# RWKV-7 in a two-block kernel: dense 64x64 products on all four quarters of the array, and the next quarter's k and r projections moved between them

## What is computed

```python
def wkv7_scan(r, w, k, v, a, b):
    def step(state, inp):
        r_t, w_t, k_t, v_t, a_t, b_t = inp
        sa = jnp.einsum('bhvk,bhk->bhv', state, a_t)
        state = (state * w_t[:, :, None, :] + sa[..., None] * b_t[:, :, None, :]
                 + v_t[..., None] * k_t[:, :, None, :])
        return state, jnp.einsum('bhvk,bhk->bhv', state, r_t)

def rwkv7_time_mix(z, mu, w0, w2, a0, a2, g2, k_k, k_a, r_k, ln_w, ln_b):
    z = z + (prev - z) * mu                      # prev: z one token earlier
    r, k, v, wd, ad, gd = split_cols(z, RWKV_SPLIT)
    decay = jnp.exp(-jnp.exp(-jax.nn.softplus(-(w0 + jnp.tanh(wd) @ w2)) - 0.5))
    a, g = jax.nn.sigmoid(a0 + ad @ a2), jax.nn.sigmoid(gd) @ g2
    kk = heads(k * k_k); kk = kk / jnp.maximum(jnp.sqrt(jnp.sum(kk * kk, axis=-1, keepdims=True)), 1e-12)
    k = k * (1.0 + (a - 1.0) * k_a)
    y = wkv7_scan(r_h, heads(decay), k_h, v_h, -kk, kk * a_h)
    # group norm of y by head, plus bonus = sum(r * k * r_k) * v, times g
```

## Time and profile before

| | us |
|---|---|
| timed runs, median of 3 | 1599.73 (1595.28 to 1599.88) |
| profiled execution | 1595.0 |
| its span | 1593.2 |
| TensorE busy in the span | 1540.0 |
| VectorE, ScalarE, GpSimd busy | 893.0, 695.6, 120.5 |

### The profile page before, as it was taken

The page is one execution under the profiler, slowest core; times in us unless marked ns, Lnnn a source line. Parts: engine busy times, 40 slices in busy tenths (PEclk is TensorE's granted clock), DMA queues, the critical chain, the costliest instruction groups (busy, mean ns, idle before and its releaser), DMA issues.

```text
span 1593.2 us, 33669 instructions
## 1 busy us (share of the span) xinstructions
PE 1540.0 (97%) x14522; PEld 1272.5 (80%) x14522; DVE 893.0 (56%) x1645; ACT 695.6 (44%) x1268; POOL 120.5 (8%) x86
## 2 busy tenths in 40 slices
PE   7999989899999999999998999999999999999998
PEld 5787757779789797887887777888887888888887
DVE  3658364656374574842245998433346677777323
ACT  5543265563352633523234998422235433333222
POOL 0004000002230322402000000000000000000000
PEclk9999989999999999999999999999999999999999
DMA  6322303431020110206312000223342323323231
GB/s 220 107 80 80 107 26 104 152 106 37 9 75 11 54 36 24 60 11 148 80 53 80 2 2 2 93 88 98 106 141 84 106 85 100 105 81 106 68 124 74
DMA packets 110947, 124.41 MB, mean 78 GB/s; under 512 B 21288, under 2 KB 94632, under 8 KB 110416
## 3 DMA queue, kind: packets, MB, share of 16 engines
q1 hardware_dynamic: 107872, 114.85, 23.3%
q10 hardware_dynamic: 2928, 7.41, 1.4%
HBM read 118.04 MB, written 4.21 MB: 77 GB/s over the span
## 4 chain that ended last, share of the span: by engine, by line
PE 76%; DVE 13%; ACT 5%; issue 3%; SPq 1%; DMA 1%; POOL 0%; DVEq 0%; ACTq 0%; POOLq 0%
PE bank L801 72%; PE bank L811 3%; ACT arena L1481 3%; DVE arena L2079 2%; DVE weights_lo L2076 2%; DVE arena L2076 2%; DVE ff_c L2079 1%; ACT L1481 1%; DVE ff_c L2076 1%; DVE act_lo L2076 1%; DVE arena L2083 1%; ACT weights_hi L1481 1%; DVE ff_c L2084 1%; DVE arena L2247 1%; DMA arena<-in_c_rwkv 1%
## 5 line engine op out<-in xcount | busy, mean ns | idle before, releaser
L1481 ACT ACTIVATE arena<-bank 128x512 f32<-128x512 f32 (+4 forms) x419 | 225.9, 566 | 564.7 <-PE bank L801 542.9
L801 PE MATMUL bank<-h_hi,weights_hi 128*128 128x512 f32 (+1 forms) x1008 | 402.4, 399 | 9.4 <-DVE weights_lo L2076 6.8
L2076 DVE TENSOR_TENSOR weights_lo<-weights,weights_hi 128x1024 fp32r<-128x1024 f32 (+1 forms) x190 | 239.6, 1261 | 305.2 <-ACT weights_hi L1481 298.2
L801 PE MATMUL bank<-h_lo,weights_hi 128*128 128x512 f32 (+1 forms) x1008 | 394.5, 391 | 0.0
L801 PE MATMUL bank<-h_hi,weights_lo 128*128 128x512 f32 (+1 forms) x1008 | 394.2, 391 | 0.0
L801 PE MATMUL bank<-arena 64*64 64x64 f32 (+7 forms) x7746 | 345.7, 247 | 16.3 <-ACT arena L1481 6.8
L801 PEld LDWEIGHTS bank<-arena 64*64 64x64 f32 (+3 forms) x7746 | 281.8, 140 | 71.2 <-issue 57.1
L1481 ACT ACTIVATE weights_hi<-weights 128x1024 fp32r<-128x1024 f32 (+1 forms) x190 | 200.2, 1054 | 167.1 <-PE bank L801 164.3
L801 PEld LDWEIGHTS bank<-h_hi,weights_hi 128*128 128x128 f32 (+1 forms) x1008 | 190.1, 189 | 60.2 <-DVE weights_lo L2076 14.2
L801 PEld LDWEIGHTS bank<-h_hi,weights_lo 128*128 128x128 f32 (+1 forms) x1008 | 190.2, 189 | 40.7
L801 PEld LDWEIGHTS bank<-h_lo,weights_hi 128*128 128x128 f32 (+1 forms) x1008 | 190.4, 189 | 37.3
(11 more groups left out here) (172 smaller groups left out, 1662.9 us busy)
## 6 DMA issues: line engine op xcount, KB each, us to landing
weights<-in_w_in SPq DMA_DIRECT2D x41, 1024.0 KB, 5.4
weights<-in_ffn_up SPq DMA_DIRECT2D x22, 1024.0 KB, 5.1
weights<-in_ffn_down SPq DMA_DIRECT2D x10, 1024.0 KB, 5.0
weights<-in_w_out SPq DMA_DIRECT2D x8, 1024.0 KB, 5.2
weights<-in_w_in SPq DMA_DIRECT2D x16, 256.0 KB, 4.6
weights<-in_w_branch_rwkv SPq DMA_DIRECT2D x4, 1024.0 KB, 5.2
weights<-in_w_branch_nsa SPq DMA_DIRECT2D x4, 1024.0 KB, 5.1
arena<-in_x SPq DMA_DIRECT2D x4, 512.0 KB, 6.3
```

Of the source, the lines that this page charges most:

```text
L801: return pe.matmul(o, w, x, start=first, stop=last)
L1481: return act.activation(o, i, f, **kw)
L2076: return dve.tensor_tensor(o, a, b, op)
```

## The change

The two head parities x (even and odd heads) become the two halves of each dense product, in place of the two halves g of the tiles. `product` takes even heads on quarters (0,0) and (1,1) and, where `cross` is set, odd heads from one half to the other, (0,1) and (1,0); the odd heads' matrices then lie in turned halves after one product and back after the next. For the parity that ScalarE reads, the old value is added on TensorE with one more product, by ident, behind each (`plus`). `ta` becomes 32 products by ident instead of 8 transposes and goes ahead of pa; `w` goes by parity too; the odd heads' first gram block is written as two products of 64 columns. ScalarE and VectorE read one parity each. GpSimd's operations are whole instead of halved, and its start of the inverse turns the odd heads.

k0, k1 and r0 of the next quarter are made in steps (`more`) at 15 places between gram and gates, r1 beside the states where k0 was. These four jobs use the last bank alone; the others go round the other seven within RWKV. The head of quarters 1 to 3 keeps v0, ss, out, v1 and kk, in this order; in it the `kk` products now stand in v1, behind the output transposes. Quarter 0's head stays, and quarter 3 has no steps.

```diff
+        beside = set()
+        first_of_rwkv = total[0]
         for q in range(4):
             if q == 0:
                 job(q, "k", 0)
             twice(q, "decay", "a")
-            job(q, "k", 1)
-            job(q, "r", 0)
-            job(q, "ss")
-            job(q, "r", 1)
-            twice(q, "kk")
-            job(q, "v", 0)
-            if q:
+            if q == 0:
+                job(q, "k", 1)
+                job(q, "r", 0)
+                job(q, "ss")
+                job(q, "r", 1)
+                twice(q, "kk")
+                job(q, "v", 0)
+                job(q, "v", 1)
+            else:
+                job(q, "v", 0)
+                job(q, "ss")
                 twice(q - 1, "out")
-            job(q, "v", 1)
+                job(q, "v", 1)
+                twice(q, "kk")
+            if q < 3:
+                for kind, n in (("k", 0), ("k", 1), ("r", 0), ("r", 1)):
+                    job(q + 1, kind, n)
+                    beside.add(J[q + 1, kind, n])
             twice(q, "tb", "tk", "low")
             for c in range(TT):
                 for x in range(2):
                     job(q, "gram", c, x)
             twice(q, "tv")
             job(q, "bonus")
...
+            for kind, lev in (("ta", None), ("pa", 0), ("pb", 0), ("pa", 1), ("pb", 1), ("pd", 1), ("pa", 2), ("pd", 2),
+                              ("pd", 3), ("mu", 0), ("mx", None), ("my", 0), ("mz", None), ("mu", 1),
+                              ("x0", None), ("my", 1)):
+                for x in range(2):
+                    job(q, kind, x, *(() if lev is None else (lev,)))
             for g in range(2):
...
+                for x in range(2):
+                    job(q, "w", x, g)
             for g in range(2):
                 for z in range(2):
                     job(q, "e", g, z)
             job(q, "g", 0)
             twice(q, "s")
             job(q, "g", 1)
...
             twice(q, "y")
             job(q, "st")
+        last_of_rwkv = total[0]
...
+        places, times, turn_of = [], [0] * BANKS, 0
+        for j in range(total[0]):
+            if j < first_of_all_banks:
+                b = j % FEW_BANKS
+            elif j in beside:
+                b = BANKS - 1
+            else:
+                if turn_of % BANKS == BANKS - 1 and first_of_rwkv <= j < last_of_rwkv:
+                    turn_of += 1
+                b = turn_of % BANKS
+                turn_of += 1
+            places.append((b, times[b]))
...
+            def product(kind, w, x, *lev, cross=True, plus=None, plus_for=()):
+
+                js = [J[(q, kind, n, *lev)] for n in range(2)]
+                for j in js:
+                    claim(pe, j)
+                for c in range(TT):
+                    for n in range(2):
+                        at_ = (2 * c + n) * DH
+                        for par in range(2):
+                            for z in range(2):
+                                rows, o = both[z], ps(js[par])[both[z ^ (par if cross else 0)], at_:at_ + DH]
+                                more = par in plus_for
+                                right = x if x is None else x[rows, c, 2 * n + par, :]
+                                ins = mm(o, w[rows, c, 2 * n + par, :], ident[rows, rows] if x is None else right, True, not more)
+                                if more:
+                                    ins = mm(o, ident[rows, rows], plus[rows, c, 2 * n + par, :], False, True)
+                            if c == TT - 1 and n == 1:
+                                fill(js[par], ins)
...
+            running = []
+
+            def more(n):
+
+                for _ in range(n):
+                    if not running:
+                        return
+                    j, k = running.pop(0)
+                    if k == 0:
+                        side.append(take_piece())
+                        claim(pe, j)
+                    ins = some_channels(j, side[-1], (k,))
+                    if k == KT - 1:
+                        fill(j, ins)
+
+            side = []
             for q in range(4):
+                if q < 3:
+                    running.extend((J[q + 1, kind, n], k) for kind, n in (("k", 0), ("k", 1), ("r", 0)) for k in range(KT))
...
+                else:
+                    w_v = take_piece()
+                    claim(pe, J[q, "v", 0])
+                    some_channels(J[q, "v", 0], w_v, range(3))
+                    pe.wait_ge(sem("kk_squares"), 2 * (q + 1))
+                    by_head(J[q, "ss"], t1_q)
+                    fill(J[q, "v", 0], some_channels(J[q, "v", 0], w_v, range(3, KT)))
                     rwkv_out(q - 1)
-                to_channels(J[q, "v", 1], h_both)
+                    w_v = take_piece()
+                    claim(pe, J[q, "v", 1])
+                    some_channels(J[q, "v", 1], w_v, range(3))
+                    pe.wait_ge(sem("kk_scale"), q + 1)
+                    for n in range(2):
+                        spread(J[q, "kk", n], kk_stat, n)
+                    fill(J[q, "v", 1], some_channels(J[q, "v", 1], w_v, range(3, KT)))
 
...
                                 if n == 1 and m == 1:
                                     fill(j, ins)
+                    more(1)
...
+                more(2)
+                pe.wait_ge(sem("powers_started"), q + 1)
+                for c in range(TT):
+                    for x in range(2):
+                        wait_read(pe, J[q, "gram", c, x])
+                product("pa", ba, pw_even, 0)
+                product("pb", pw_even, ba, 0)
+                more(2)
+                settled("pa", 0)
+                settled("pb", 0)
+                product("pa", pwt, pw_odd, 1)
+                product("pb", pw_odd, pwt, 1)
+                pe.wait_ge(sem("inv_started"), q + 1)
+                product("pd", pw_odd, invt, 1, plus=invt, plus_for=(1,))
+                more(2)
+                settled("pa", 1)
+                settled("pb", 1)
+                product("pa", pwt, pw_even, 2)
+                settled("pd", 1)
+                product("pd", pw_even, invt, 2, plus=invt, plus_for=(1,))
+                more(2)
+                settled("pa", 2)
+                settled("pd", 2)
+                product("pd", pw_odd, invt, 3, plus=invt, plus_for=(1,))
+                more(2)
+                settled("pd", 3)
+                pe.wait_ge(sem("between_ready"), 2 * q + 1)
+                product("mu", e_m[0], invt, 0)
+                product("mx", invt, None)
+                more(2)
+                settled("mu", 0)
+                settled("mx")
+                product("my", inv, mid, 0, plus=invt, plus_for=(0,))
+                product("mz", mid, inv, cross=False, plus=inv, plus_for=(1,))
+                more(1)
+                settled("my", 0)
+                pe.wait_ge(sem("between_ready"), 2 * q + 2)
+                product("mu", e_m[1], invt, 1)
+                pe.wait_ge(sem("v_centred"), q + 1)
+                product("x0", ka, v_by_head)
+                more(2)
+                settled("mu", 1)
+                settled("mz")
+                product("my", inv, mid, 1, plus=invt, plus_for=(0,))
+                more(2)
+                settled("my", 1)
+                settled("x0")
```

On ScalarE, VectorE and GpSimd (cut):

```diff
@@ ScalarE @@
+                if q == 0:
+                    mix_of(q, "k", 1)
+                    stream_to(J[q, "r", 0])
...
+                if q == 0:
+                    mix_of(q, "r", 0)
+                    stream_to(J[q, "r", 1])
+                else:
                     root("gn", q - 1, stat[:, 56:72], stat[:, 56:72])
...
                 mix_of(q, "v", 1)
+                if q < 3:
+                    stream_to(J[q + 1, "k", 1], 0)
...
+                to_parity(J[q, "pa", 0, 0], pw_odd, 0)
+                to_parity(J[q, "pb", 0, 0], pwt, 0)
+                if q < 3:
+                    mix_of(q + 1, "k", 0, 0)
+                else:
+                    stream_to(base["kcvc"])
+                to_parity(J[q, "pa", 0, 1], pw_even, 0)
+                to_parity(J[q, "pb", 0, 1], pwt, 0)
+                to_parity(J[q, "pd", 1, 1], invt, 1)
+                if q < 3:
+                    stream_to(J[q + 1, "r", 0], 0)
...
@@ VectorE @@
                 if q:
+                    stream_to(J[q, "v", 1], 0)
                     norm_sums(q - 1)
...
                 mix_of(q, "v", 1)
+                if q < 3:
+                    stream_to(J[q + 1, "k", 1], 0)
...
+                to_parity(J[q, "pa", 1, 0], pw_odd, 1)
+                to_parity(J[q, "pb", 1, 0], pwt, 1)
...
+                if q < 3:
+                    mix_of(q + 1, "k", 0, 0)
+                to_parity(J[q, "pa", 1, 1], pw_even, 1)
+                to_parity(J[q, "pb", 1, 1], pwt, 1)
+                dve.wait_ge(sem("inv_started"), q + 1)
+                sum_into(J[q, "pd", 0, 1], invt, 0)
...
@@ GpSimd @@
+                pool.tensor_tensor(whole(pw_even), whole(low), over(m_blk, 16), ALU.mult).then_inc(sem("powers_started"), 1)
...
```

(50 more changed lines are left out.)

351 lines of the change are left out of this document (139 added, 212 removed).

## The result

The changed kernel takes 1656.2 us (median of 4 runs, 1651.74 to 1659.05), the kernel before 1599.8 beside it: ratio 1.0363, 95% interval 1.0337 to 1.0389. It is slower by 56 us. The forecast was 1637: 41.6 us on top of the profiled execution's 1595.0, or 37 above the median before. The profiled execution took 1651.7, its span is 1649.9.

A forecast was written before the change was run, and what follows sets the result against it. TensorE, busy 97% of the span, was taken as the bound. Quarter 0 +12.3, quarters 1 and 2 +15.2 each, quarter 3 -1.1: +41.6 us on 1595.0, so 1637; range 1604 to 1658.

The forecast's parts named there:

- -4: Quarter 3, without steps: 9.2 us saved on products and w, less five exposed waits for evictions, net -4.
- rival D: Dense products with addend: the addend blocks, up to 9.4 us more a quarter, total 1645 to 1674; chance 0.10.
- the mechanism of the head: Heads of quarters 1 to 3: 16.5 us of TensorE work leaves, yet other engines' chain keeps the length; TensorE idles.
- Rival A: Heads of quarters 1 to 3: they follow TensorE's work, 16.5 us off each, total about 1578; chance 0.10.
- (a): Dense products: crossing halves plain groups to 0.93 us, addend groups gain nothing, mz takes 2.8; saves 7.45 us a quarter.
- C: Crossed products: row tiles collide on a bank, so crossing does nothing; +41 us, total 1678; chance 0.04.
- the rule of one bank for two row halves: Crossed pairs: the skill says different row tiles cannot access one PSUM bank simultaneously, so no gain; "y" rows contradict it.
- (b): "w" products, crossed by halves: saves 1.75 of 3.50 us a quarter; "ta" costs about as its eight transposes.
- (c): 24 projection steps at 15 places in quarters 0 to 2: 16.4 us of work plus 4.5 for the places, a quarter.
- (d): Gram stretch: its hole goes, -1.4 us, and a new wait for the new k piece's low half comes, +2.0.
- The new wait for the low piece: First step after gram: TensorE waits for VectorE to make the new k piece's low half, +2.0 us.
- The head and its clock: Heads of quarters 1 to 3: +0.4 us from the chain through "out", +2.5 from half clock after 8.5 us idle.

The follow-up runs named there:

- e2: Changed kernel with v1 and the kk products issued ahead of the "out" transposes in the heads of quarters 1 to 3: 1637.3 us, ratio 1.0250 to the kernel before.
- e10: Kernel before with only the w products crossed by parity and the first gates product between w and e: 1594.5 us, ratio 0.9991 to the kernel before.
- e3: Changed kernel with the kernel before's head and no steps between dense products, leaving the crossing by head parity alone: 1627.1 us, ratio 1.0182 to the kernel before.
- m1: Separate small kernel timing 64x64 fp32 products on TensorE in four stretches, without the computation: 1024 crossed products took 57.0 us, 1024 uncrossed 60.
- e1: Changed kernel with its dense products not crossed, w and ta still crossed: 1682.2 us, ratio 1.0532 to the kernel before.
- e5: Kernel of e3 with its dense products not crossed: 1641.2 us, ratio 1.0283 to the kernel before.
- m2: Second separate small kernel timing four stretches of other record kinds, without the computation; 1024 crossed bf16 products of 64 columns took 27.5 us.
- Stretch C: Stretch of m2 with 512 uncrossed fp32 products, each followed by a bf16 product of 8 columns: 81.9 us.

## Why the prediction came out as it did

By quarter, from the profiles, measured against forecast: rests +12.6, +16.2, +18.2, +12.2 against +12.3, +12.3, +12.3, -4; heads -0.2, -0.3, -0.3 against +2.9 each. Sum 58.4 against 41.6. (The span grew by 56.7: 1.7 us came off outside the quarters.)

**In range by luck.** 1656.2 lies 2 us inside the range of 1604 to 1658 and 1 us beyond the 1612 to 1655 that got the chance of 0.63. Only rival D, 1645 to 1674, has the number within its span, and its mechanism didn't occur. The price that made most of the miss, the supply of instructions, stands nowhere in the sum or among the rivals; the heads, 9.5 us cheaper than forecast, kept the total in range.

**The side, and the mechanism of the head, were right.** The head did not follow TensorE's work: 11 us of work left it and it stayed as long, with holes ahead of ss (4.84) and "out" (4.21), and e2 shows the queue order behind it as named. Rival A is out.

**(a) and C.** A plain crossed group takes 0.93 start to start, an addend group 1.91 to 1.93, mz 2.8, as forecast; the rule of one bank for two row halves, which the prediction quotes, cost nothing here, where each pair writes separate partitions. So the occupancies were right, and rivals C and D are out. What (a) lacked was a second price: 353 more records in a rest (2129 for 1776), 72 of them wide ones of the steps and 281 small ones, each owing 27.8 ns of supply, 9.8 us for all. The saved 7.45 us come out in full only where wide products stand beside them.

**(b)** saves 1.2 to 1.9 us a quarter of TensorE's work in e10, for the 1.75 of the sum, and three quarters of four give it back.

**(c)** overpriced: steps cost 16.4 + 4.5 in my sum, and 5 to 8 us in the traces on top of e3 (about 10 by the medians), 13.5 to 15 where nothing is crossed. In quarter 0 this error and the missing price of supply cancelled (12.6 for 12.3), which is luck too.

**(d) is the step that failed by its reading.** I took the hole of 1.4 us in the gram stretch for a wait that the change would remove. The timeline of the kernel before has it as

```profile
469.79 1.31 PE L801 MATMUL bank<-arena 64*64 64x128 f32 x36 [1.44 <-issue]
```

and it was the one stop on the supply that the old kernel had in that quarter: it ends 2.3 us behind the start of a packet at 467.46, as the stops of m1 do. It was the sign that the small products already ran within 5% of the supply (29.2 ns a record for 27.8). Such stops didn't go; they multiplied, the waits on issue from 4 to 18 between 330 and 810 us. The new wait for the low piece was 1.05 (forecast 2.0).

**Quarter 3 is the term most mis-sized**, by 16.2 us, as much as the whole miss of 16.8; the other rests (+10.1) and the heads (-9.5) cancel. "-4" was 9.2 saved less 5.2 for evictions. The evictions came as forecast: five waits of 0.75 to 1.09, 4.9 us for 5.2. But the waits on issue rose from 1.1 to 9.6 us, and without steps the crossing brought next to nothing (e1, q3: 70.99 for 71.53; e5 for e3: 73.37 for 71.26). Taking away what occupancy gives for it, 9 plain and 5 addend groups by 0.93, turns -4 into +9. Of the other 3, 1.3 are a wait on VectorE in the gram stretch that the sum had at nothing (1.51 at 712.68, for 0.17 at 666.21 before). The rest is not shown; the clock, 0.95 for 0.98, was lower as well.

**The head and its clock.** Forecast 0.4 and 2.5 longer, measured 0.2 shorter. The chain to "out" was 1.4 us shorter than I made it (21.8 for 23.2), and ss and the rest of v0, at half clock, ended 2.9 later (17.6 us behind decay for 14.7): so TensorE waited 4.2 there and not 8.5. The half clock cost 1.5 to 1.6 behind "out" and nothing at ss, where 2.5 was forecast.

## What to carry to other kernels

Price a stream of small products twice: by the array's quarters, and by the count of instructions (here 27 to 28 ns for each matmul with its weight load, in blocks of 128). Crossing paid here mostly where few, wide instructions stood nearby to let the supply catch up, and the stops that it made elsewhere brought stretches at half clock as well. A lone idle "issue" of one to two microseconds in a stretch of small instructions is a sign that this limit may be near, above all if it ends a fixed time behind an instruction packet. Before moving work out of a full engine's way, ask how long the other chain there is, and put what gates that chain first in the queue.

## What was not expected of the hardware

- After a wait, 351 records ran before the first stop, in 7.4 us; then exactly 128 at a time, 3.4 to 4.0 us apart (m1).
- The limit holds at half clock too: 1024 bf16 records in 27.5 us at a granted 0.59 (m2, B). Stretch C behind it, busy throughout, was granted 0.50 for its whole 81.9 us.
- Stops of 1 to 2 us in a stretch of small products were enough for the half clock: 3.71 us busy of 6.80, then 13.6 us at 0.50 (e3, quarter 3).
- With the same products in the rest of quarter 0, four kernels take 74.59 to 80.18 us there; the longest had a granted clock of 0.96 and the others 1.00.
